# A split-precision transformer kernel on one core: weights in equal 1 MB chunks, with deeper slots and earlier splits

## The chip, the core and the metric

The kernel runs on one core of a Trainium2 chip. The metric is the device time of one execution in microseconds. A core has TensorE (PE in the profile), VectorE (DVE), ScalarE (ACT), GpSimd (POOL) and SyncE (SP), each with its own program; they meet at semaphores.

## What is computed

Two blocks on x of 256 tokens by 1024. The first has four layers (differential attention, stick-breaking attention, sliding-window attention, differential attention again), each followed by an output projection and a gated feed-forward network with a causal convolution; then a norm. The second has one layer with a pooling mixer beside attention, and at its end a gated embedding.

```python
for layer in range(DEPTH):                      # 4
    h = rmsnorm(x, attn_norm[layer])
    m = diff_attention | stick_breaking_attention | sliding_window_attention (h)
    x = x + m @ w_o[layer]
    h = rmsnorm(x, ffn_norm[layer])
    x = x + conv_gated_ffn(h, ffn_w_up[layer], ..., ffn_w_down[layer])
x = rmsnorm(x, final_norm)
# second block
proj = rms_norm(x, g_mix_pre) @ w_in
y = concat(pool_mixer(u), moba_attention(q, k, v)) @ w_out
x = x + rms_norm(y, g_mix_post)
x = x + rms_norm(conv_ffn(rms_norm(x, g_ffn_pre), w_up, conv_w, conv_b, w_down), g_ffn_post)
x = x + (p @ w_ple) * sigmoid(x @ w_ple_gate)
```

## The kernel before

All products are in fp32 made of two parts: every operand is rounded to a high half (type fp32r) and its remainder, the low half, and a product is three matmuls of 128x128 by 256 columns (`product`, L1568 to L1570) or, in the down stages of layers 0 to 3, one of 256 (L1578) and one of 512 columns (L1579, `wide_product`). The weights pass once through the core: SyncE loads a chunk from HBM into `w_raw`, ScalarE casts it into `w_hi` (L351), VectorE subtracts into `w_lo` (L863), TensorE multiplies. All three are rings of RING = 3 slots of 2816 columns. A chunk of an attention, wo or up stage is 2048 columns (1 MB), one of a down stage 2816 (one output tile, 22 units of 128 rows), one of the gate stage 2560.

The stages follow each other in the list `STAGES`: attention, wo, up, down for each of five layers, then gate. Every engine's program walks through it, and between its other work `next_split(c0, k)` casts or subtracts chunk c0+k+3, once TensorE has done with chunk c0+k (semaphore `used`, waited for by ScalarE). VectorE's program waits for `hi_ready`, SyncE's and TensorE's for `lo_ready`. TensorE begins a chunk with `chunk_ready` (L1583). A split is thus at a fixed place in each engine's program; where it stands, the engine's later work waits for it.

In a down stage VectorE adds each tile to x (L1369, L1372) as soon as TensorE is done with it, ScalarE squares the tile (L383, in down3 also L382), VectorE sums the squares into `acc` (L902, then L904) and subtracts the next chunk. TensorE does most of the first two tiles, then their rest once the last activations are there, and then one tile after the other. The split of the last tile is postponed until after the next normalisation.

A norm's statistic is a matmul of `acc` with ones (L1696) and of the last squares (L1700, `statistic`); TensorE has begun the next stage's first outputs by then, on x that is scaled but not normalised yet (h from `raw_high`, ACT L419, and `raw_low`, DVE L925). ScalarE makes rstd (L396), VectorE normalises (L916, low halves L912), for the chunks behind. In a wo stage the fourth chunk is split in halves (ACT L359, DVE L872), `added_to_x` adds the tiles (L1265), and the second and third splits stand among the squares. In layer 4 the result of wo is normed itself and then added (L1005, L1014), in a stage that the names call res_a.

In the attention groups of two heads (`group`), ScalarE makes exponentials (`exps`, L435), copies transposed probabilities (`copy_probT`, L443), and TensorE's `heads` (L1732) multiply these with the values. In the gate stage two `embedding` products stand ahead of the gate's first outputs. The repeating parts of the stages are hardware loops (`Fori`) on all engines.

## Time and profile before

| | |
|---|---|
| time of three runs | 1567.25, 1567.72, 1568.3 us (median 1567.72) |
| time of the profiled execution | 1566.53 us |
| its span in the profile | 1564.9 us |
| TensorE's matmuls (PE) | busy 1515.5 us, 11578 instructions |
| VectorE (DVE) | busy 1052.2 us |
| ScalarE (ACT) | busy 867.5 us |
| GpSimd (POOL) | busy 324.0 us |
| read from HBM | 262.50 MB |
| mean granted TensorE clock | 0.991 |

Times are microseconds from the start of the span. An engine is busy while it executes an instruction. A bracket at the end of a row of a timeline says how long the engine sat idle before and what released it. The difference between the execution's time and its span is 1.6 us.

### The profile page before, as it was taken

To read this page: it belongs to the slowest core of one execution; us is meant where nothing else is said; L and a number is where in the kernel's file an instruction comes from. 1 tells how busy PE (TensorE), PEld (TensorE's weight loads), DVE (VectorE), ACT (ScalarE), POOL (GpSimd) and SP (SyncE) were. 2 spreads that over 40 slices of the span, in tenths; PEclk is the share of its full clock that TensorE was granted. 3 is DMA by queue.
4 is the path that set the end of the run, shared out by engine and by line. 5 is a ranking of instruction groups with operands and counts; after the bars stand their busy time and mean duration, and the time that the engine had idled before them with its cause. 6 is when DMAs were issued, how large, how long until landed. Compare 5 with 4: busy or idle time off the path is not lost.

```text
span 1564.9 us, 31081 instructions
## 1 busy us (share of the span) xinstructions
PE 1515.5 (97%) x11578; PEld 1436.4 (92%) x11578; DVE 1052.2 (67%) x1677; ACT 867.5 (55%) x1365; POOL 324.0 (21%) x482
## 2 busy tenths in 40 slices
PE   8999999999999999989999999999999998899998
PEld 7989999899999998978999889889998887899998
DVE  6668877563378775666877576678785765866545
ACT  6766555465566554555656446666564555544533
POOL 2003212212222222212211221022112361211100
PEclk9999999999999999999999999999999998899999
DMA  7543656353336564442556545435564553455550
GB/s 263 185 149 115 209 187 240 139 186 116 126 108 215 183 223 158 161 163 81 195 182 222 180 165 172 150 127 201 182 233 148 170 173 108 143 182 196 192 208 28
DMA packets 37242, 264.65 MB, mean 169 GB/s; under 512 B 4959, under 2 KB 5274, under 8 KB 8496
## 3 DMA queue, kind: packets, MB, share of 16 engines
q1 hardware_dynamic: 33984, 255.54, 46.8%
q0 software_dynamic: 3040, 8.05, 2.0%
q8 instruction: 49, 0.80, 0.2%
q14 instruction: 25, 0.20, 0.0%
q10 hardware_dynamic: 144, 0.05, 0.0%
HBM read 262.50 MB, written 1.12 MB: 168 GB/s over the span
## 4 chain that ended last, share of the span: by engine, by line
PE 77%; DVE 13%; ACT 6%; issue 3%; DMA 1%; SPq 0%; ACTq 0%; POOL 0%; DVEq 0%
PE bank L1568 19%; PE bank L1569 19%; PE bank L1570 19%; PE bank L1579 9%; PE bank L1578 4%; DVE w_lo L863 4%; DVE tmp L916 2%; ACT w_hi L351 2%; ACT tmp L435 1%; PE bank L1617 1%; PE bank L1732 1%; DVE acc L904 1%; DVE tmp L948 1%; DVE h_lo L912 1%; DVE w_lo L872 1%
## 5 line engine op out<-in xcount | busy, mean ns | idle before, releaser
L863 DVE TENSOR_TENSOR w_lo<-w_raw,w_hi 128x2048 fp32r<-128x2048 f32 (+2 forms) x219 | 542.0, 2477 | 211.2 <-ACT w_hi L351 211.0
L1568 PE MATMUL bank<-h_hi,w_hi 128*128 128x256 f32 x2016 | 574.5, 285 | 2.2 <-DVE w_lo L863 2.2
L1569 PE MATMUL bank<-h_lo,w_hi 128*128 128x256 f32 x2016 | 570.4, 283 | 0.0
L1570 PE MATMUL bank<-h_hi,w_lo 128*128 128x256 f32 x2016 | 570.3, 283 | 0.0
L351 ACT CAST w_hi<-w_raw 128x2048 fp32r<-128x2048 f32 (+2 forms) x219 | 443.4, 2025 | 2.8 <-DVE proj L932 2.8
L1568 PEld LDWEIGHTS bank<-h_hi,w_hi 128*128 128x128 f32 x2016 | 386.5, 192 | 7.4 <-issue 3.5
L1569 PEld LDWEIGHTS bank<-h_lo,w_hi 128*128 128x128 f32 x2016 | 386.7, 192 | 0.1
L1570 PEld LDWEIGHTS bank<-h_hi,w_lo 128*128 128x128 f32 x2016 | 386.6, 192 | 0.0
L1579 PE MATMUL bank<-act_both,w_hi 128*128 128x512 f32 x704 | 248.9, 399 | 0.0
L800 ACT ACTIVATE tmp<-bank,par 128x256 f32<-128x256 f32 x181 | 93.4, 561 | 227.6 <-PE bank L1570 227.3
L1332 DVE SCALAR_TENSOR_TENSOR tmp<-bank,par,tmp 128x255 f32<-128x255 f32 (+1 forms) x362 | 155.4, 477 | 85.0 <-ACT tmp L800 82.3
L1578 PE MATMUL bank<-act_both,w_lo 128*128 128x256 f32 x704 | 197.7, 281 | 0.0
L1579 PEld LDWEIGHTS bank<-act_both,w_hi 128*128 128x128 f32 x704 | 132.3, 188 | 32.7
L1568 PE MATMUL bank<-act_both,w_hi 128*128 128x256 f32 x516 | 150.6, 292 | 6.7 <-DVE act_both L1020 5.1
L1569 PE MATMUL bank<-act_both,w_hi 128*128 128x256 f32 x516 | 146.6, 284 | 0.0
L1570 PE MATMUL bank<-act_both,w_lo 128*128 128x256 f32 x516 | 146.5, 284 | 0.0
L1539 POOL CAST act_both<-tmp 128x256 f32 x110 | 43.6, 397 | 481.0 <-DVE tmp L1349 371.1
L1578 PEld LDWEIGHTS bank<-act_both,w_lo 128*128 128x128 f32 x704 | 133.0, 189 | 0.0
L1568 PEld LDWEIGHTS bank<-act_both,w_hi 128*128 128x128 f32 x516 | 99.3, 192 | 13.2 <-DVE act_both L1020 7.0
L1617 PE MATMUL bank<-h_hi,w_hi 128*128 128x256 f32 x336 | 94.4, 301 | 5.9 <-ACT h_hi L419 2.9
L1569 PEld LDWEIGHTS bank<-act_both,w_hi 128*128 128x128 f32 x516 | 99.5, 193 | 0.1
L1570 PEld LDWEIGHTS bank<-act_both,w_lo 128*128 128x128 f32 x516 | 99.5, 193 | 0.0
(185 smaller groups left out, 2037.6 us busy)
## 6 DMA issues: line engine op xcount, KB each, us to landing
w_raw<-w_std SPq DMA_DIRECT2D x180, 1024.0 KB, 4.9
w_raw<-w_down SPq DMA_DIRECT2D x40, 1408.0 KB, 6.1
act_both<-vec_dram POOLq DMA_DIRECT2D x56, 128.0 KB, 3.6
w_raw<-w_gate SPq DMA_DIRECT2D x4, 1280.0 KB, 5.4
x<-xT SPq DMA_DIRECT2D x2, 512.0 KB, 6.0
out<-x SPq DMA_DIRECT2D x3, 256.0 KB, 2.3
w_raw<-w_std SPq DMA_DIRECT2D x2, 256.0 KB, 5.4
w_raw<-w_std SPq DMA_DIRECT2D x1, 512.0 KB, 8.0
```

What stands on the lines that cost most here:

```text
L351: act.copy(w_hi[:, slot, 0:width], w_raw[:, slot, 0:width]).then_inc(hi_ready, 1)
L800: act.activation(to[:, slot, :], source, ACT.Identity, bias=col(3), scale=col(2)).then_inc(conv_init, 1)
L863: dve.tensor_tensor(w_lo[:, slot, 0:width], w_raw[:, slot, 0:width], w_hi[:, slot, 0:width].bitcast(F32), ALU.subtract).then_inc(lo_ready, 1)
L916: dve.scalar_tensor_tensor(hf[:, k, :], x[:, k, :], gain_of(app, k), rstd[:, :], ALU.mult, ALU.mult).then_inc(hf_done, 1)
L1332: return dve.scalar_tensor_tensor(to[:, slot, lag:S], source(v)[:, 0:S - lag], par[:, bass.ds(at + (4 * v + 2 - lag), 1)], to[:, slot, lag:S],
L1539: pool.tensor_copy(act_hi[:, bass.ds(j, 1), :].squeeze(1) if not isinstance(j, int) else act_hi[rows, j, :], cval[rows, slot, :]).then_inc ...
L1568: pe.matmul(dst, wh, xh, start=first, stop=False, skip_group_check=shared)
L1569: pe.matmul(dst, wh, xl, start=False, stop=False, skip_group_check=shared)
L1570: done = pe.matmul(dst, wl, xh, start=False, stop=last, skip_group_check=shared)
L1578: pe.matmul(bank[:, 0:S], wl, xh, start=start and k == 0, stop=False, skip_group_check=True)
L1579: done = pe.matmul(bank[:, :], wh, pair, start=False, stop=stop and k == len(weights) - 1, skip_group_check=True)
L1617: pe.matmul(dst, a, b, start=k == 0 and w is wh and (n == 0 or not shared), stop=False, skip_group_check=shared)
```

## The change

All weights come in chunks of 1 MB: a down stage has 11 of them instead of 8 (a tile of 22 units crosses chunk borders), the gate's weights four and the embedding's one of its own. `w_raw` has three slots, `w_hi` and `w_lo` have SLOTS = 5. Splits are counted in chunks of weights: `split_to(c)` makes all that are missing up to c, and `ahead(c, lead)` those up to lead beyond the stage's chunk c. ScalarE's lead is mostly one more than VectorE's (`HIGH`, `high_up`, `low_up`); in down both are at 5. ScalarE waits for `used` of the chunk that had the slot. In the last group of an attention stage both engines make extra splits; a wo stage has one split, behind the first addition to x, and one after the normalisation; nothing is split in halves and nothing postponed. In `group`, `copy_probT(s, 0)` stands ahead of the next exponentials. In the gate stage all four embeddings stand first. All hardware loops are written out. New lines: splits ACT L363 and DVE L841, additions in down DVE L1326 and L1329, sums of squares DVE L870 and L872, in wo L1232, `product` PE L1522 to L1524, `wide_product` PE L1532 and L1533.

```diff
@@ -58,17 +56,33 @@
 
 
 STAGES = []
-SIZES = []
-for _kind, _count, _width in (
-        ("da", 12, STD), ("wo", 4, STD), ("up", FT, STD), ("down", DT, DOWN),
-        ("sb", 12, STD), ("wo", 4, STD), ("up", FT, STD), ("down", DT, DOWN),
-        ("sw", 6, STD), ("wo", 4, STD), ("up", FT, STD), ("down", DT, DOWN),
-        ("da", 12, STD), ("wo", 4, STD), ("up", FT, STD), ("down", DT, DOWN),
-        ("mix", 9, STD), ("wo", 4, STD), ("up", FT, STD), ("down", DT, DOWN),
-        ("gate", 4, GATE)):
-    STAGES.append((_kind, len(SIZES), _count))
-    SIZES += [_width] * _count
-CHUNKS = len(SIZES)
+_at = 0
+for _kind, _count in (
+        ("da", 12), ("wo", 4), ("up", FT), ("down", DT),
+        ("sb", 12), ("wo", 4), ("up", FT), ("down", DT),
+        ("sw", 6), ("wo", 4), ("up", FT), ("down", DT),
+        ("da", 12), ("wo", 4), ("up", FT), ("down", DT),
+        ("mix", 9), ("wo", 4), ("up", FT), ("down", DT),
+        ("gate", 4)):
+    STAGES.append((_kind, _at, _count))
+    _at += _count
+SLOTS = 5
+AHEAD = 5
+HIGH = 4
+RAW = 3
+UNITS = STD // P
+DOWN = FT * DT // UNITS
+
+
+WEIGHTS = []
+FIRST_WEIGHTS = {}
+for _kind, _first, _count in STAGES:
+    FIRST_WEIGHTS[_first] = len(WEIGHTS)
+    if _kind == "down":
+        WEIGHTS += [_first + (UNITS * _j + UNITS - 1) // FT for _j in range(DOWN)]
+    else:
+        WEIGHTS += ([_first] if _kind == "gate" else []) + [_first + _j for _j in range(_count)]
+CHUNKS = len(WEIGHTS)
 EXP_AND_LN = 6
 WINDOWS = (2, 4, 8, 16)
...
 
+        def weights_of(layer, c):
+
+            return c + (DOWN - DT) * layer + (layer == 5)
+
+        def weight_slot(layer, c):
+            return weights_of(layer, c) % SLOTS
+
+        def high_up(j):
+
+            return min(AHEAD, RING + (j + 1) // 2)
+
+        def low_up(j):
+
+            return min(AHEAD - 1, RING + j // 4)
+
+        def down_weights(c0, k):
+
...
+            split = [1]
+
+            def split_to(c):
+
+                for n in range(split[0], min(c + 1, CHUNKS)):
+                    if n >= SLOTS:
+                        act.wait_ge(used, WEIGHTS[n - SLOTS] + 1)
+                    act.wait_ge(arrived[n % RAW], n // RAW * 16 + 16)
+                    act.copy(w_hi[:, n % SLOTS, :], w_raw[:, n % RAW, :]).then_inc(hi_ready, 1)
+                    split[0] = n + 1
+
+            def ahead(c, lead=RING):
+
+                split_to(weights_of(layer, c) + lead)
 
...
@@ -560,13 +550,13 @@
 
                             q, s, d, t = (i * 2 + half, i * 2 + s_half, i * 2 + d_half, i * 2 + first_tile)
                             at = i * RING + (g0 + RING)
-                            reg = i if not isinstance(i, int) else None
-                            off = g0 + RING + (i * RING if isinstance(i, int) else 0)
+                            copy_probT(s, 0, maps)
                             exps(s + 1, 1, 0)
                             if more:
                                 evac_qk(at, slot_of(g0, 0), 0)
-                            copy_probT(s, 0, maps)
                             head_squares(q, d, 0) if da else mix_high(q, t)
+                            if not more and da:
+                                ahead(c0 + n, HIGH)
                             if not more and not da:
                                 act.wait_ge(used, at + 1)
                                 for g in range(4):
@@ -574,20 +564,20 @@
...
@@ -736,19 +727,13 @@
                             for k in tiles:
                                 raw_high(app, k)
 
-                    split_hi_halves(c0)
-                    if layer < 4:
-                        next_split(c0, 1)
+                    ahead(c0, AHEAD)
                     squared(0)
                     raw(0, 1)
                     squared(1)
-                    if layer == 4:
-                        next_split(c0, 1)
...
-                n = c0 + k + RING
-                if i is None and n >= CHUNKS:
-                    return
-                split_lo(n if i is None else i * RING + n, n % RING, SIZES[n])
+            split = [1]
+
+            def split_to(c):
+
+                for n in range(split[0], min(c + 1, CHUNKS)):
+                    dve.wait_ge(hi_ready, n + 1)
+                    dve.tensor_tensor(w_lo[:, n % SLOTS, :], w_raw[:, n % RAW, :],
+                                      w_hi[:, n % SLOTS, :].bitcast(F32), ALU.subtract).then_inc(lo_ready, 1)
+                    split[0] = n + 1
+
...
@@ -1266,10 +1233,9 @@
                            .then_inc(x_part if k == 3 else bank_free, 1)
 
                     added_to_x(0)
-                    split_lo_halves(c0, layer)
+                    ahead(c0, AHEAD)
                     added_to_x(1)
                     added_to_x(2)
-                    next_split(c0, 1)
                     for j in range(3):
                         add_squares(name, j)
                         if layer < 4:
@@ -1279,19 +1245,16 @@
                     if layer < 4:
                         raw_low(app, 6)
                         raw_low(app, 7)
-                        next_split(c0, 2)
                         normalise(app, SUMS[name][2])
-                        next_split(c0, 3)
...
@@ -1302,7 +1265,7 @@
                         dve.wait_ge(conv_part, (j + ffn * FT) * 3 + 3)
                         dve.scalar_tensor_tensor(cgate[:, slot, 2:S], pj[slot][:, 0:S - 2], par[:, at:at + 1],
                                                  cgate[:, slot, 2:S], ALU.mult, ALU.add).then_inc(bank_free, 1)
-                        next_split(c, 0)
+                        split_to(weights_of(layer, c) + low_up(j))
                         dve.wait_ge(gated, j + ffn * FT + 1)
                         dve.tensor_tensor(cval[0:HALF, slot, :], cgate[0:HALF, slot, :], cval[0:HALF, slot, :],
...
@@ -1376,7 +1333,7 @@
                         if layer < 4 and raw_engine(app, k):
                             raw_low(app, k)
                         if k < DT - 1:
-                            next_split(c0, k)
+                            split_to(down_weights(c0, k) + AHEAD)
                     if layer == 4:
                         dve.wait_ge(p_hi, 1)
...
-                    def down(c, slot, a=0, b=FT):
-
+                    first = FIRST_WEIGHTS[c0]
+
+                    def down_tile(f, k):
+
+                        n, at = divmod(f * FT + k, UNITS)
+                        return w_tile((first + n) % SLOTS, at, P, 0)
+
+                    def down(f, a=0, b=FT):
+
+                        pe.wait_ge(lo_ready, first + (f * FT + b - 1) // UNITS + 1)
                         if a == 0:
-                            chunk_ready(c)
-                        weights = [w_tile(slot, k, P, 0) for k in range(a, b)]
+                            pe.wait_ge(bank_free, c0 + f + 1)
+                        bank = pj[slot_of(c0, f)]
+                        weights = [down_tile(f, k) for k in range(a, b)]
                         if layer < 4:
...
@@ -2062,32 +2017,33 @@
                     layer += 1
                 else:
                     def embedding(k):
-                        slot = slot_of(c0, k)
+
+                        for t in range(2):
+                            done = product(embedded[k][:, t * S:t * S + S],
+                                           [w_tile(ple % SLOTS, 2 * k + f, 2 * P, t * P) for f in range(2)],
+                                           [(act_hi[:, f, :], act_lo[:, f, :]) for f in range(2)])
+                        return done
+
+                    ple = FIRST_WEIGHTS[c0]
+                    pe.wait_ge(lo_ready, ple + 1)
+                    pe.wait_ge(p_lo, 1)
+                    for k in range(4):
+                        embedding(k)
+                    for k in range(n):
+                        slot, weights = slot_of(c0, k), weight_slot(layer, c0 + k)
                         chunk_ready(c0 + k)
-                        for t in range(2):
-                            product(val_bank[k % 3][:, t * S:t * S + S],
-                                    [w_tile(slot, DT + f, 2 * P, t * P) for f in range(2)],
-                                    [(act_hi[:, f, :], act_lo[:, f, :]) for f in range(2)])
-
-                    pe.wait_ge(p_lo, 1)
```

VectorE, wo stage of layer 0, from the first addition to x to the first of the normalisation (L1265/L1232 adds to x, L904/L872 sum squares, L925/L893 low halves of h). Before:

```order
L872 TENSOR_TENSOR w_lo<-w_raw,w_hi 128x1024 [waits half_hi]
L872 TENSOR_TENSOR w_lo<-w_raw,w_hi 128x1024 [waits hi_ready]
L1265 TENSOR_TENSOR x<-bank,x 128x512 [waits used] x2
L863 TENSOR_TENSOR w_lo<-w_raw,w_hi 128x2048 [waits hi_ready]
L904 TENSOR_TENSOR acc<-sq 128x256 [waits acc_done,sq_ready]
L925 SCALAR_TENSOR_TENSOR h_lo<-x,par,h_hi 128x256 [waits raw_hi]
L904 TENSOR_TENSOR acc<-acc,sq 128x256 [waits acc_done,sq_ready]
```

```order
L1265 TENSOR_TENSOR x<-bank,x 128x256 [waits tile6_done]
L1265 TENSOR_TENSOR x<-bank,x 128x256 [waits used]
L925 SCALAR_TENSOR_TENSOR h_lo<-x,par,h_hi 128x256 [waits raw_hi] x2
L863 TENSOR_TENSOR w_lo<-w_raw,w_hi 128x2048 [waits hi_ready]
L916 SCALAR_TENSOR_TENSOR tmp<-x,par,rstd 128x256 [waits rstd_done]
```

And now:

```order
L1232 TENSOR_TENSOR x<-bank,x 128x512 [waits used]
L841 TENSOR_TENSOR w_lo<-w_raw,w_hi 128x2048 [waits hi_ready]
L1232 TENSOR_TENSOR x<-bank,x 128x512 [waits used] x2
L872 TENSOR_TENSOR acc<-sq 128x256 [waits acc_done,sq_ready]
L893 SCALAR_TENSOR_TENSOR h_lo<-x,par,h_hi 128x256 [waits raw_hi]
L872 TENSOR_TENSOR acc<-acc,sq 128x256 [waits acc_done,sq_ready]
```

```order
L893 SCALAR_TENSOR_TENSOR h_lo<-x,par,h_hi 128x256 [waits raw_hi]
L1232 TENSOR_TENSOR x<-bank,x 128x256 [waits tile6_done]
L1232 TENSOR_TENSOR x<-bank,x 128x256 [waits used]
L893 SCALAR_TENSOR_TENSOR h_lo<-x,par,h_hi 128x256 [waits raw_hi] x2
L884 SCALAR_TENSOR_TENSOR tmp<-x,par,rstd 128x256 [waits rstd_done]
```

Of four splits between the first addition and the normalisation (two halves, two whole) one whole is left, in the halves' place.

VectorE, the start of the down stage of layer 0, behind the last row of up. Before:

```order
L1307 TENSOR_TENSOR tmp<-tmp 64x256 [waits gated]
L1369 TENSOR_TENSOR x<-bank,x 128x256 [waits used]
L1372 TENSOR_TENSOR x<-bank,x 128x256 [waits x_main]
L902 COPY acc<-sq 128x256 [waits acc_done,sq_ready]
L863 TENSOR_TENSOR w_lo<-w_raw,w_hi 128x2816 [waits hi_ready]
L1369 TENSOR_TENSOR x<-bank,x 128x256 [waits used]
L1372 TENSOR_TENSOR x<-bank,x 128x256 [waits x_main]
```

And now:

```order
L1270 TENSOR_TENSOR tmp<-tmp 64x256 [waits gated]
L1326 TENSOR_TENSOR x<-bank,x 128x256 [waits used]
L1329 TENSOR_TENSOR x<-bank,x 128x256 [waits x_main]
L870 COPY acc<-sq 128x256 [waits acc_done,sq_ready]
L841 TENSOR_TENSOR w_lo<-w_raw,w_hi 128x2048 [waits hi_ready] x2
L1326 TENSOR_TENSOR x<-bank,x 128x256 [waits used]
L1329 TENSOR_TENSOR x<-bank,x 128x256 [waits x_main]
```

The third tile's weights were a chunk split in up; now they end in the stage's fifth chunk, the first of the two L841 behind the COPY. TensorE, end of the second tile and start of the third (its first row waits for `bank_free` and `lo_ready`), now:

```order
L1533 MATMUL bank<-act_both,w_hi 128x512
L1532 MATMUL bank<-act_both,w_lo 128x256
L1533 MATMUL bank<-act_both,w_hi 128x512
L1532 MATMUL bank<-act_both,w_lo 128x256 [waits bank_free,lo_ready]
L1533 MATMUL bank<-act_both,w_hi 128x512
```

ScalarE, last group of the mix layer (L435/L433 exponentials, L443/L441 the copy, L449/L447 heads' results, L574/L564 the pooled). Before:

```order
L483 COPY vtok<-bank 128x512 [waits pv_done,used]
L351 CAST w_hi<-w_raw 128x2048 [waits arrived2,used]
L435 ACTIVATE tmp,small<-tmp,small 128x128 [waits nmax_ready]
L435 ACTIVATE tmp,small<-tmp,small 128x256
L435 ACTIVATE tmp,small<-tmp,small 128x128
L435 ACTIVATE tmp,small<-tmp,small 128x256
L443 COPY tmp<-bank 128x384 [waits trans_done]
L443 COPY tmp<-bank 128x384
L449 CAST act_both<-bank 128x256 [waits pv_done]
L574 ACTIVATE act_both<-bank,par 128x256 [waits used]
```

And now:

```order
L481 COPY vtok<-bank 128x512 [waits pv_done,used]
L363 CAST w_hi<-w_raw 128x2048 [waits arrived0,used]
L441 COPY tmp<-bank 128x384 [waits trans_done]
L441 COPY tmp<-bank 128x384
L433 ACTIVATE tmp,small<-tmp,small 128x128 [waits nmax_ready]
L433 ACTIVATE tmp,small<-tmp,small 128x256
L433 ACTIVATE tmp,small<-tmp,small 128x128
L433 ACTIVATE tmp,small<-tmp,small 128x256
L447 CAST act_both<-bank 128x256 [waits pv_done]
L564 ACTIVATE act_both<-bank,par 128x256 [waits used]
```

The copy for the first head moved ahead of the four exponentials of the second, and stands right behind the cast.

## Rows read from the trace of the kernel before

**Rows 1.** The page: part 1 (busy time), part 4 (chain), shares by engine.

```profile
PE 1515.5 (97%) x11578; PEld 1436.4 (92%) x11578; DVE 1052.2 (67%) x1677; ACT 867.5 (55%) x1365; POOL 324.0 (21%) x482
...
PE 77%; DVE 13%; ACT 6%; issue 3%; DMA 1%; SPq 0%; ACTq 0%; POOL 0%; DVEq 0%
```

**Rows 2.** Timeline of PE, gate stage; start us, us, engine line op, [idle before <-releaser].

```profile
1533.52 0.28 PE L1617 MATMUL bank<-h_hi,w_hi 128*128 128x256 f32 x1
1533.64 0.28 PE L1617 MATMUL bank<-h_hi,w_lo 128*128 128x256 f32 x1
```

**Rows 3.** Timeline of PE, first down stage: the third tile's first matmuls.

```profile
276.39 0.28 PE L1578 MATMUL bank<-act_both,w_lo 128*128 128x256 f32 x1
...
276.75 0.28 PE L1578 MATMUL bank<-act_both,w_lo 128*128 128x256 f32 x1
```

**Rows 4.** PE's waits, whole span; us in total, times, longest us.

```profile
PE bank L1732 <- ACT tmp L443: 6.5, 6, 1.6
PE bank L1696 <- DVE acc L904: 5.7, 5, 2.0
...
PE bank L1700 <- ACT sq L383: 5.0, 5, 2.2
PE bank L1568 <- DVE w_lo L863: 4.2, 9, 0.6
...
PE bank L1626 <- DVE h_lo L912: 1.6, 6, 0.4
...
PE bank L1568 <- DVE w_lo L872: 0.2, 1, 0.2
```

**Rows 5.** Timeline of PE, layer 0's attention, first and last group.

```profile
46.17 0.45 PE L1732 MATMUL bank<-tmp,vtok 128*128 128x256 f32 x1 [0.80 <-ACT tmp L443]
...
111.76 0.45 PE L1732 MATMUL bank<-tmp,vtok 128*128 128x256 f32 x1 [1.25 <-ACT tmp L443]
```

**Rows 6.** Timelines of ACT and PE, last group of the mix layer.

```profile
1290.88 0.46 ACT L443 COPY tmp<-bank 128x384 f32<-128x384 f32 x1
...
1291.81 0.70 PE L1732 MATMUL bank<-tmp,vtok 128*64 128x256 f32 x2 [2.42 <-issue]
```

**Rows 7.** Timeline of DVE, wo of layer 0.

```profile
128.11 2.28 DVE L863 TENSOR_TENSOR w_lo<-w_raw,w_hi 128x2048 fp32r<-128x2048 f32 x1
```

**Rows 8.** Groups of DVE by form: busy us, mean ns, idle before.

```profile
L863 DVE TENSOR_TENSOR w_lo<-w_raw,w_hi 128x2048 fp32r<-128x2048 f32 x175 | 405.0, 2317 | 134.7 <-ACT w_hi L351 134.4
L863 DVE TENSOR_TENSOR w_lo<-w_raw,w_hi 128x2816 fp32r<-128x2816 f32 x40 | 125.8, 3144 | 68.9 <-ACT w_hi L351 68.9
```

**Rows 9.** Timeline of DVE, wo of layer 4.

```profile
1329.02 2.29 DVE L863 TENSOR_TENSOR w_lo<-w_raw,w_hi 128x2048 fp32r<-128x2048 f32 x1 [0.75 <-ACT w_hi L351]
```

**Rows 10.** Timeline of PE, gate stage: the last of the first 48 matmuls.

```profile
1540.71 0.40 PE L1626 MATMUL bank<-h_lo,w_hi 128*128 128x256 f32 x2
```

**Rows 11.** Windows; busy us of PE, PEld, DVE, ACT, POOL, then PEclk, DMA share, GB/s.

```profile
448.10:451.80 3.70, 2.11 (x10) 1.08 (x8) 2.89 (x7) 2.30 (x5) 2.58 (x4) 1.00 0.40 168
451.90:455.20 3.30, 3.30 (x16) 3.21 (x16) 3.30 (x5) 2.89 (x4) 0.00 (x0) 0.50 0.00 0
1291.80:1294.90 3.10, 3.09 (x15) 2.46 (x16) 1.02 (x4) 1.50 (x5) 0.00 (x0) 0.50 0.76 254
1229.00:1231.80 2.80, 0.73 (x2) 0.00 (x0) 2.02 (x3) 0.71 (x2) 0.93 (x2) 1.00 1.01 198
152.00:266.00 114.00, 114.00 (x939) 113.35 (x938) 90.72 (x125) 68.15 (x84) 23.32 (x42) 1.00 0.59 201
```

**Rows 12.** Timeline of DVE: first tile's squares in down, layers 0 and 4.

```profile
276.90 0.29 DVE L902 COPY acc<-sq 128x256 f32<-128x256 f32 x1 [0.48 <-ACT sq L383]
...
1480.44 0.29 DVE L902 COPY acc<-sq 128x256 f32<-128x256 f32 x1 [8.71 <-ACT sq L383]
```

**Rows 13.** Timeline of PE, down of layer 4: the third tile's start.

```profile
1481.02 0.28 PE L1569 MATMUL bank<-act_both,w_hi 128*128 128x256 f32 x1
```

**Rows 14.** Timeline of ACT, first group of layer 1's attention.

```profile
342.60 1.91 ACT L351 CAST w_hi<-w_raw 128x2048 fp32r<-128x2048 f32 x1
```

404 lines of the change are left out of this document (154 added, 250 removed).

## The prediction

> **What bounds the kernel now.** I began with the busy shares and the chain of waits [rows 1]. TensorE is busy for 1515.5 of 1564.9 us, and 77% of the chain is TensorE's own work, 19% is VectorE's and ScalarE's. The matmuls are the same before and after, so only the time that TensorE does not spend at full rate can change. Beside each other, 256-column matmuls start every 0.12 us [rows 2]. In the down stages of the first four layers, a pair (256 and 512 columns) takes 0.36 us [rows 3]. Then the list of TensorE's waits [rows 4] says what it waited for: attention copies, the statistic of a norm, low halves of weights. I take each of them in turn. The profiled execution took 1566.53 us, 1.2 below the median of 1567.72; the sum goes by it, and 1.2 is added at the end. About 0.2% (3.1 us) is what a measurement can tell from no change.
>
> **What should be gained.**
> 1. Attention groups. In the differential layers ScalarE now copies the first transposed probabilities ahead of the next exponentials. The three waits of TensorE for that copy [rows 4, 5] are 0.80 in the first group of layer 0, 1.25 in its last and 1.6 in layer 3; I keep 0.3 for what is next in line and take 3.4. In the last group of the mix layer the copy stands behind four exponentials: it starts at 1290.88, TensorE's heads at 1291.81 after a wait of 2.42 [rows 6]. The copy needs only the transposes, which had ended at 1288.4. I take 2.4, and 0.8 (half) of what the slow clock behind this wait costs (below): 3.2.
> 2. The wo stages of layers 0 to 3. VectorE has a split of 2.28 at 128.11 ahead of the statistic's sums [rows 7] and another just ahead of the normalisation (order of VectorE ahead, first place); neither is there any more. TensorE waited for the sums 0.9 in each of the four layers (5.7 in five waits less the 2.0 of wo4) and for the last squares 0.7 each (5.0 less the 2.2 of down3) [rows 4], 6.5 in all. Next in line is the addition of the last tile to x and its square, which stay; I leave 0.3 per layer to them and take 5.2. Of the 1.6 for low halves of h (L912) I take 1.1.
> 3. Weights that come late. Nine waits for w_lo of L863 and one of L872 make 4.4 [rows 4]: the third chunk after a down stage, whose split was postponed, and the third chunk of up, whose split follows the normalisation. With five slots both are split well ahead: 4.4.
> 4. At the end of down3 a 2816-column subtraction (3.14) [rows 8] stands in each tile's round, and the last squares come 2.2 late [rows 4]. The pieces are now 2048 wide (2.32), and the last round has one or none of them: 2.6, with the idle piece behind it.
> 5. wo4: a cast and then a subtraction (2.29 after 0.75 idle) [rows 9] stand in VectorE's chain of x, sums and h; they are gone, and the chain is what all waits there hang on: 3.0.
> 6. The end: the gate's first 48 matmuls run from 1533.52 [rows 2] to 1540.95, two starts after the last row's [rows 10], where 48 x 0.12 is 5.8: they wait for h. Two more embeddings (24 matmuls, 2.9) now stand ahead and fill these 1.7.
> 7. Clock: 451.90 to 455.20 ran at a granted clock of 0.50 [rows 11], the 1.2 GHz level, after TensorE had been busy 2.11 of the 3.70 us before. At half clock matmuls start every 0.213 us, so 3.3 us do the work of 1.8: 1.5 lost, and gained once the two waits before it are.
>
> Sum: 3.4 + 3.2 + 5.2 + 1.1 + 4.4 + 2.6 + 3.0 + 1.7 + 1.5 = 26.1.
>
> **What should be lost.**
> 1. **A new wait at the third tile of every down stage.** Tile 2 needs units 44 to 65, that is chunks 2 to 4 of the stage. Up leaves four of them subtracted; the fifth follows on VectorE only behind the first tile's two additions and the COPY of its squares (order of VectorE ahead, second place). In the trace of before these end at 276.90 + 0.29 = 277.2 [rows 12], for they wait for the first tile's matmuls. Then comes a subtraction of 2.3 (the 2048-wide mean is 2.32): 279.5. TensorE begins tile 2 at 276.39 [rows 3] (44 pairs after the stage's first). So 3.1 us in each of layers 0 to 2; in layer 3 the squares are two ACTIVATEs, 0.6 more, 3.7; in layer 4 the COPY ends at 1480.73 [rows 12], the subtraction at 1483.0, and TensorE gets there at 1481.0 [rows 13]: 2.0. In all 3 x 3.1 + 3.7 + 2.0 = 15.0. Before, tile 2 had a chunk of its own that was ready, so no wait. ScalarE's cast is no help: it is done in up already. The next tile is safe: its chunk is the second subtraction, ready 2.3 later, while tile 2 takes 22 x 0.36 = 7.9.
> 2. The slow clock behind these waits. No row shows a wait of 3.1 after a long dense stretch. The nearest: after the 2.42 before 1291.8 the clock was 0.50 for 3.1 us, after 2.8 us with 0.73 busy (1229.0 to 1231.8) it stayed 1.00 [rows 11]. Bounds 0 and 5 x 1.5 = 7.5; I take three of five, 4.5. The Trainium skill (TensorE: Matmul & The Clock Gate, "The HAM clock gate") says that an idle TensorE falls to 1.2 GHz and must be kept fed; by it alone all five would fall and the loss would be 7.5, and the rows so far show it after some gaps and not after others.
> 3. Stick-breaking's first group: its cast of 1.9 right ahead of the logarithms [rows 14] is two casts now. TensorE has the first chunks of group 1 to do meanwhile, so of 1.9 some 1.1 should show (0 to 1.9).
>
> Sum: 15.0 + 4.5 + 1.1 = 20.6.
>
> **What costs nothing.** Loads: some 240 loads of 1 MB instead of 225 of 1 to 1.4 MB; each waits for a slot far ahead of need, and TensorE's list has no wait for weights from memory. The splits that move into the last heads lie where VectorE waits for the last squares and heads (it idles for a third of the span); if that cover were gone, each would cost up to 2.3 before wo, 11.5 at most over five stages. The five w_hi and w_lo slots: without price. Unrolling: in the up stage of layer 0, with its loop turns, 939 recorded matmuls take 114.0 us [rows 11], and 939 x 0.12 is 112.7, so at most 1.3 us are there to gain. I take 0.
>
> Net 26.1 - 20.6 = 5.5 less: 1561.0 on the profiled execution, **1562.2** on the median.
>
> **Rivals.**
> - *The down wait shows nothing* (the fifth chunk is ready by another way than I read, or TensorE is late there for another reason): 1562.2 - 15.0 - 4.5 = 1542.7. Against it: the wait on lo_ready stands in the program and VectorE's order is fixed. Chance 0.09.
> - *Slower: the gains at the statistics fall to the next in line.* In wo0 to wo3 and at down3 and wo4 the last addition to x, its square and the copy to acc follow each other across VectorE and ScalarE, and cutting 2.3 us of split ahead of them gains only if they start earlier. If the last matmuls set their start, gain terms 2 (5.2 + 1.1), 4 and half of 5 fall away, 10.4, and with all five clocks down 3.0 more is lost: 1562.2 + 13.4 = 1575.6. It decides slower once 8.7 (1570.9 - 1562.2) of the gains are missing. For it: L1265 adds the last two tiles behind TensorE's own last matmuls of wo. Against: the wait for the sums (0.9) came before. Chance 0.13.
> - *Unrolling pays.* If each of the five up stages had 1.3 to give, it would be 1562.2 - 6.5 = 1555.7. The Trainium skill (Runtime: NRT & Kernel Launch, "Instruction fetch mechanics") says that a taken branch outside the two pages held breaks the sequential prefetch and that unrolling avoids it; no gap stands at a loop's turn here. Chance 0.08.
> - *The clock alone is misjudged*: none or all of the five: 1557.7 or 1565.2. Chance 0.20, in both cases with my mechanism.
> - The forecast as it stands: 0.50.
>
> **How the numbers follow.** The forecast's own bounds: 0 to 1.9 for the logarithms, 0 to 7.5 for the clock, and the gains to within a fifth (5) give 1553 to 1571. The slower rival with half its price ends at 1569; a quarter of the cases beyond either end is left out, so 1550 to 1572. Faster (below 1564.6): the first rival, the third, half of the clock's and 0.35 of the forecast's 0.50, 0.62. Slower (above 1570.9): 0.13. The same: 0.25.
>
> **What would show it.** In the profile after: a wait of the 256-column matmul for w_lo at the third tile of each down stage, about 3.1 four times and 2.0 in layer 4, and PEclk 0.5 behind some of them. The waits for acc and for w_lo at the third chunks are gone, the wait of the heads for the copy of the probabilities too. VectorE's split stands at 2.32 mean with no 3.14. I would be wrong if the down stages had no wait, or if TensorE still waited for sums in wo.

## The result, and the profile after

The changed kernel takes 1571.19 us (median of 19 runs, 1566.15 to 1572.51), the kernel before 1568.3 us beside it (19 runs, 1566.78 to 1570.06). The ratio is 1.0015, with an interval from 1.0009 to 1.0021: slower by some 2.4 us. That is little, but it lies clear of 1 on the side that I had not forecast: I had forecast 1562.2, or 5.5 less. The profiled execution took 1569.87 us with a span of 1568.2.

The page after, its span, busy times and chain:

```profile
span 1568.2 us, 28431 instructions
...
PE 1515.6 (97%) x11578; PEld 1440.5 (92%) x11578; DVE 1053.3 (67%) x1688; ACT 868.8 (55%) x1376; POOL 337.0 (21%) x482
...
PE 82%; DVE 8%; ACT 6%; issue 2%; POOL 1%; DMA 1%; SPq 0%; ACTq 0%
```

TensorE's work is as before [rows 1]: 1515.6 us of 11578 matmuls. GpSimd's 324.0 has become 337.0, though it does the same 482 instructions: its masks in the stick-breaking layer took 17.9 us and take 22.2, and its scalings of x (L1441 before, L1395 now), for which no wait of TensorE is listed, took 47.7 and take 60.0. TensorE's waits after (line, what it waited for; us in total, times, longest):

```profile
PE bank L1532 <- DVE w_lo L841: 12.1, 4, 3.4
PE bank L1834 <- POOL tmp L1467: 8.0, 6, 2.4
PE bank L1522 <- DVE act_both L988: 5.0, 3, 2.2
...
PE bank L1522 <- DVE w_lo L841: 4.1, 7, 1.9
PE bank L1689 <- ACT tmp L441: 3.1, 5, 1.1
...
PE bank L1657 <- ACT sq L381: 1.9, 4, 0.5
PE bank L1653 <- DVE acc L872: 1.9, 2, 1.2
```

Against [rows 4]: the copy of the probabilities (L443, 6.5 us) is at 3.1, the sums (L904, 5.7) at 1.9, the last squares (L383, 5.0) at 1.9, and the wait of 2.42 in the mix layer [rows 6] is gone (0.3 of issue is left of it). Two waits are new: 12.1 us for the low halves of weights at the third tile of four down stages (L1532; layer 4's own, 1.9, is in the L1522 row of 4.1), and 8.0 us for GpSimd's masks in the stick-breaking layer (L1834). The first I had forecast. The second I had not: in the kernel before it is 0.7 us.

The forecast wait, in the down stage of layer 0 (VectorE's COPY and its two subtractions, then TensorE's third tile):

```profile
272.01 0.29 DVE L870 COPY acc<-sq 128x256 f32<-128x256 f32 x1 [0.48 <-ACT sq L381]
272.22 4.49 DVE L841 TENSOR_TENSOR w_lo<-w_raw,w_hi 128x2048 fp32r<-128x2048 f32 x2
...
274.56 0.38 PE L1532 MATMUL bank<-act_both,w_lo 128*128 128x256 f32 x1 [2.90 <-DVE w_lo L841]
```

The COPY ends at 272.30, the first subtraction at 274.50, and TensorE starts at 274.56 after 2.90 idle. The five waits are 2.90 in layers 0 to 2, 3.43 in layer 3 and 1.93 in layer 4. Behind four of them TensorE's clock is halved. Windows of the trace after, columns as in [rows 11]:

```profile
600.60:604.00 3.40, 3.40 (x12) 2.91 (x11) 1.93 (x4) 1.94 (x3) 3.02 (x4) 0.50 0.93 371
883.90:887.30 3.40, 3.40 (x12) 2.88 (x11) 2.88 (x4) 0.75 (x3) 3.27 (x2) 0.50 0.84 279
1191.10:1194.50 3.40, 3.40 (x12) 2.92 (x11) 2.48 (x4) 1.44 (x4) 2.71 (x3) 0.50 0.87 330
1484.60:1488.00 3.40, 3.40 (x18) 3.40 (x17) 3.40 (x3) 1.39 (x1) 0.00 (x0) 0.50 0.86 287
274.40:277.80 3.40, 3.24 (x19) 2.87 (x20) 3.06 (x4) 0.27 (x1) 3.32 (x2) 1.00 0.70 212
```

The four windows at 0.50 are at 1.2 GHz, the last of them behind the wait of only 1.93; the one behind the first wait is not, although that wait is 2.90. In the whole trace 10 stretches add up to 41.3 us at half clock; before they were 7 with 29.7.

The other new wait, second group of the stick-breaking layer. VectorE's softplus (L1169) and subtraction (L841), GpSimd's masks (L1467), TensorE:

```profile
375.04 1.02 DVE L1169 SCALAR_TENSOR_TENSOR tmp<-bank,tmp 128x384 f32<-128x384 f32 x2 [1.39 <-ACT tmp L625]
375.98 2.28 DVE L841 TENSOR_TENSOR w_lo<-w_raw,w_hi 128x2048 fp32r<-128x2048 f32 x1
...
375.67 3.58 POOL L1467 TENSOR_SCALAR_AFFINE_SELECT tmp<-tmp 128x256 f32<-128x256 f32 x4 [1.54 <-DVE tmp L1169]
...
378.58 0.48 PE L1834 MATMUL bank<-tmp,cst 128*128 128x256 f32 x1 [1.41 <-POOL tmp L1467]
```

The same place before (L1206 is the softplus, L1513 the masks, then ScalarE's cast):

```profile
373.70 1.02 DVE L1206 SCALAR_TENSOR_TENSOR tmp<-bank,tmp 128x384 f32<-128x384 f32 x2 [1.19 <-ACT tmp L636]
...
374.33 0.87 POOL L1513 TENSOR_SCALAR_AFFINE_SELECT tmp<-tmp 128x256 f32<-128x256 f32 x2 [1.34 <-DVE tmp L1206]
376.35 0.79 POOL L1513 TENSOR_SCALAR_AFFINE_SELECT tmp<-tmp 128x256 f32<-128x256 f32 x2 [1.14 <-ACT tmp L643]
...
376.54 1.90 ACT L351 CAST w_hi<-w_raw 128x2048 fp32r<-128x2048 f32 x1
```

Before, the two masks behind the softplus take 0.87 us, and the next two at 376.35 take 0.79. After, VectorE starts the subtraction at 375.98, in the middle of the masks, and the row of masks from 375.67 is 3.58 long. The instruction alone, over all groups (ns min/median/max), after:

```profile
L1467 POOL TENSOR_SCALAR_AFFINE_SELECT tmp<-tmp x32: 402/407/2397, 345.6 to 433.6; 128x256 f32<-128x256 f32 x32
```

The median is 0.407 us, the longest 2.397. In each of the four groups one mask begins 0.15 us after a subtraction of 2.28 or 2.29 has begun, takes 2.39 to 2.40 and ends 0.26 after it; two more begin 1.30 after one and take 1.25, again to 0.26 after its end. So a mask that begins while a subtraction runs stands still until the subtraction is over. A mask that was already running when one began (348.02, the subtraction at 348.33) took its 0.41.

### The profile page after: what moved, and what is told of

The parts are those of the page before. It is cut to its first block, busy times and chain, and to the rows that moved or that the text cites. A ratio compares the mean times of both kernels' runs of the same rounds, so it can differ in the third digit from the quotient of the medians.

```text
span 1568.2 us, 28431 instructions
## 1 busy us (share of the span) xinstructions
PE 1515.6 (97%) x11578; PEld 1440.5 (92%) x11578; DVE 1053.3 (67%) x1688; ACT 868.8 (55%) x1376; POOL 337.0 (21%) x482
## 4 chain that ended last, share of the span: by engine, by line
PE 82%; DVE 8%; ACT 6%; issue 2%; POOL 1%; DMA 1%; SPq 0%; ACTq 0%
PE bank L1522 20%; PE bank L1524 19%; PE bank L1523 19%; PE bank L1533 10%; PE bank L1532 5%; ACT w_hi L363 2%; DVE w_lo L841 2%; PE bank L1571 2%; DVE tmp L884 2%; PE bank L1580 1%; PE bank L1689 1%; DVE acc L872 1%; POOL tmp L1467 1%; ACT tmp L433 1%; PE bank L1657 1%
## 5 line engine op out<-in xcount | busy, mean ns | idle before, releaser
L841 DVE TENSOR_TENSOR w_lo<-w_raw,w_hi 128x2048 fp32r<-128x2048 f32 x240 | 556.5, 2326 | 91.8 <-ACT w_hi L363 91.6
L1522 PE MATMUL bank<-h_hi,w_hi 128*128 128x256 f32 x2016 | 574.8, 285 | 1.9 <-DVE w_lo L841 1.9
L1524 PE MATMUL bank<-h_hi,w_lo 128*128 128x256 f32 x2016 | 570.5, 283 | 0.0
L363 ACT CAST w_hi<-w_raw 128x2048 fp32r<-128x2048 f32 x240 | 454.5, 1903 | 73.1 <-DMA w_raw<-w_std 59.6
L1522 PEld LDWEIGHTS bank<-h_hi,w_hi 128*128 128x128 f32 x2016 | 386.8, 192 | 7.1 <-issue 3.5
L1524 PEld LDWEIGHTS bank<-h_hi,w_lo 128*128 128x128 f32 x2016 | 386.7, 192 | 0.0
L1533 PE MATMUL bank<-act_both,w_hi 128*128 128x512 f32 x704 | 251.8, 401 | 0.0
L1532 PE MATMUL bank<-act_both,w_lo 128*128 128x256 f32 x704 | 200.0, 284 | 12.1 <-DVE w_lo L841 12.1
L1533 PEld LDWEIGHTS bank<-act_both,w_hi 128*128 128x128 f32 x704 | 134.3, 191 | 31.9
L1522 PE MATMUL bank<-act_both,w_hi 128*128 128x256 f32 x516 | 150.8, 292 | 7.8 <-DVE act_both L988 5.0
L1532 PEld LDWEIGHTS bank<-act_both,w_lo 128*128 128x128 f32 x704 | 135.3, 192 | 13.4 <-DVE w_lo L841 13.4
L1524 PE MATMUL bank<-act_both,w_lo 128*128 128x256 f32 x516 | 146.9, 285 | 0.0
L1522 PEld LDWEIGHTS bank<-act_both,w_hi 128*128 128x128 f32 x516 | 99.8, 193 | 13.4 <-DVE act_both L988 6.3
L381 ACT ACTIVATE sq<-x 128x256 f32<-128x256 f32 (+1 forms) x62 | 29.3, 474 | 139.9 <-DVE x L1329 119.2
L1395 POOL TENSOR_SCALAR proj<-x,par 128x256 f32<-128x256 f32 x33 | 49.8, 1509 | 255.3 <-ACT h_hi L417 254.8
```

The lines of the kernel that those rows point to most:

```text
L363: act.copy(w_hi[:, n % SLOTS, :], w_raw[:, n % RAW, :]).then_inc(hi_ready, 1)
L841: dve.tensor_tensor(w_lo[:, n % SLOTS, :], w_raw[:, n % RAW, :], w_hi[:, n % SLOTS, :].bitcast(F32), ALU.subtract).then_inc(lo_ready, 1)
L1395: pool.tensor_scalar(proj[:, k % 4, :], x[:, k, :], gain_of(app, k), None, ALU.mult)\
L1522: pe.matmul(dst, wh, xh, start=first, stop=False, skip_group_check=shared)
L1524: done = pe.matmul(dst, wl, xh, start=False, stop=last, skip_group_check=shared)
L1532: pe.matmul(bank[:, 0:S], wl, xh, start=start and k == 0, stop=False, skip_group_check=True)
```

## The experiments

Each one was timed beside the kernel before; ratios are to that kernel, differences are of medians, "against the changed kernel" means against its 1571.19.

### The fifth subtraction of down ahead of the additions

```diff
                 elif kind == "down":
                     name = f"down{layer}"
+                    split_to(FIRST_WEIGHTS[c0] + AHEAD - 1)
                     for k in range(DT):
```

> The changed kernel, with VectorE's fifth subtraction of each down stage moved ahead of the stage's first addition (it stood behind the first tile's additions and the COPY of its squares). My theory: the wait of TensorE at the third tile (12.1 us in four waits and 2.1 in layer 4) goes entirely and with it four stretches of half clock (4 x 1.5 us): 14.9 + 6 = some 19 to 21 us less than the changed kernel, ratio to the kernel before about 0.989. Rival A, that ScalarE's casts or the loads set that chunk: the wait stays at 2 us or more per stage and the time moves by less than 5. Rival B, that the half clock comes anyway: 15 less, and the stretches near 600, 884, 1191 and 1485 stay.

Measured: 1549.64 us, ratio 0.9871 (0.9856 to 0.9886), 21.5 less than the changed kernel. VectorE at the start of down now:

```profile
270.59 0.42 DVE L1327 TENSOR_TENSOR x<-bank,x 128x256 f32<-128x256 f32 x1 [6.34 <-PE bank L1534]
271.05 0.42 DVE L1330 TENSOR_TENSOR x<-bank,x 128x256 f32<-128x256 f32 x1
271.95 0.29 DVE L870 COPY acc<-sq 128x256 f32<-128x256 f32 x1 [0.48 <-ACT sq L381]
274.16 2.29 DVE L841 TENSOR_TENSOR w_lo<-w_raw,w_hi 128x2048 fp32r<-128x2048 f32 x1 [1.91 <-ACT w_hi L363]
```

No subtraction that the third tile needs stands behind the COPY any more; what comes at 274.16 is the sixth chunk. Of TensorE's waits none for w_lo is left at the wide products; those for the masks are as they were, and the other ones for w_lo are without layer 4's:

```profile
PE bank L1835 <- POOL tmp L1468: 8.1, 6, 2.4
...
PE bank L1523 <- DVE w_lo L841: 1.9, 5, 0.4
```

The four stretches of half clock are gone with the waits (the trace has 6 left, 24.2 us). My theory holds, rivals A and B fall. The gaps at the third tiles, beyond the usual spacing of matmuls, were 3.06 three times, 3.59 and 2.09, or 14.9; with four stretches of 3.4 us at half speed (an estimate of 1.5 each, 6.0) that is 20.9 of the 21.5. The spans of the two profiled executions differ by 20.2.

### VectorE's subtractions behind the masks

```diff
                             softplus(b, 0)
                             softplus(b, 1)
+                            mix_low(q, i * 2)
                             if more:
                                 ahead(at)
                                 ahead(at + 1)
                             else:
                                 ahead(c0 + n)
                                 ahead(c0 + n, HIGH)
-                            mix_low(q, i * 2)
                             mix_low(q + 1, i * 2 + 1)
```

> The changed kernel, with VectorE's two subtractions in each stick-breaking group moved from ahead of the first low half of the heads' results to behind it; ScalarE's order is untouched. Theory: GpSimd's masks (0.41 us alone, up to 2.40 in the changed kernel) stand still while VectorE subtracts 2048 columns beside them; with the subtraction behind, masks take 0.41 again and TensorE's 8.0 us of waits for them go, with one half-clock stretch (1.5): 8 to 9.5 less than the changed kernel, ratio to before about 0.996. Rival, that ScalarE's extra cast ahead of the logarithms delays the masks: the waits of about 1.6 to 2.5 per group stay, time the same within 2 us.

`mix_low` makes the low half of a head's result; its first call now stands between the softplus and the subtractions.

Measured: 1560.29 us, ratio 0.9948 (0.9934 to 0.9961), 10.9 less. The masks in this kernel:

```profile
L1467 POOL TENSOR_SCALAR_AFFINE_SELECT tmp<-tmp x32: 406/406/410, 348.0 to 427.8; 128x256 f32<-128x256 f32 x32
```

Every one takes 0.41. TensorE's waits for them fell from 8.0 to 1.7 us. ScalarE's order is that of the changed kernel, casts ahead of the logarithms included, so the rival falls as the main cause.

### ScalarE's lead back to three in the stick-breaking groups

```diff
                             if more:
-                                ahead(at, HIGH)
+                                ahead(at)
...
                             if more:
-                                ahead(at + 1, HIGH)
+                                ahead(at + 1)
...
-                                ahead(at + 2, HIGH)
+                                ahead(at + 2)
...
-                        ahead(g0 + 2, HIGH)
+                        ahead(g0 + 2)
```

> The changed kernel, with ScalarE's lead in the stick-breaking groups back from four chunks to three; VectorE's order is untouched, and its subtraction waits for the cast as before. Theory of the masks: the subtraction can't start before the masks are done, so the masks are short and TensorE's 8.0 us of waits go: 8 to 9.5 less, ratio about 0.996. If only one of this run and of the one with VectorE's subtractions moved brings it, the order of ScalarE (this one) or the overlap (the other) is the cause; if both do, it is the overlap.

Measured: 1559.61 us, ratio 0.994 (0.9927 to 0.9954), 11.6 less. TensorE's wait for masks is 0.6 us. Here VectorE's order is untouched. Both moves bring it, and what they share is that the subtraction no longer meets the masks that TensorE waits for. From the first to the last matmul that waited for masks in the changed kernel (346.53 to 430.65, 84.1 us) the same matmuls now take 74.4, 9.7 less: 7.2 of waits, the stretch of half clock at 351.4 (an estimate of 1.5), and the rest not told apart. The other 1.9 of the 11.6 fell elsewhere.

This also says where the overlap came from. In the kernel before VectorE's subtraction stood at the same place in its program, but it waited for a cast that ScalarE began at 376.54 (above) and ended at 378.45; the two masks from 376.35 were done by 377.14. The subtraction then ran from 378.48 and stalled the next mask, for which TensorE did not wait. The lead of four had the cast done early, the wait on `hi_ready` was over before it began, and the subtraction ran at once, into the masks that TensorE waits for.

### The loops of the kernel before written out

```diff
-                            with act.Fori(0, groups - 1) as i:
+                            for i in range(0, groups - 1):
```

and so at all loops of TensorE, ScalarE and VectorE.

> The kernel before with the hardware loops of TensorE, ScalarE and VectorE written out, as in the change, and nothing else. My forecast: no difference, 0 within 2 us (ratio 0.999 to 1.001), since no gap stood at a loop's turn. Rival, that turns cost: 4 to 8 us less. Rival, that the longer program costs (twice the instruction fetches): 2 to 5 more.

Measured: 1567.77 us, ratio 0.9991 (0.9982 to 1.0), 0.9 less. At most a small gain; the rival of 4 to 8 falls, and so does a cost of 2 to 5. The two profiled executions differ by more than that inside: TensorE's waits add up to 41.1 us against 45.2 before, and its half clock to 40.8 us against 29.7. So the 0.9 is what is left of both; the price of the loops without the clock was not measured.

### The copy of the probabilities first, in the kernel before

```diff
+                            copy_probT(s, 0, maps)
                             exps(s + 1, 1, 0)
                             if more:
                                 evac_qk(at, slot_of(g0, 0), 0)
-                            copy_probT(s, 0, maps)
```

> The kernel before with only the copy of the first head's transposed probabilities put ahead of the next exponentials. My terms for this part: 3.4 in the differential layers and 3.2 in the mix layer, 6.6 less, ratio 0.996, with the wait of 2.42 at 1291.8 and its half clock gone. Rival: the exponentials behind the copy are late in turn and TensorE waits for the divided probabilities instead: within 2 us of before.

Measured: 1562.03 us, ratio 0.9963 (0.995 to 0.9977), 6.2 less. TensorE's waits for the copy, 6.5 before:

```profile
PE bank L1732 <- ACT tmp L443: 2.8, 3, 1.1
```

The wait of 2.42 in the mix layer is gone and no stretch of half clock stands behind it. A wait of 1.2 for divided probabilities (L987) is new, the rival in small.

### Both repairs together

> The changed kernel with both repairs: the fifth subtraction of a down stage ahead of its additions, and ScalarE's lead of three in the stick-breaking groups. If the two losses are independent, their measured savings add up (21.5 and 11.6 by the medians of their own runs against the changed kernel's 1571.2): 1538, ratio to before 0.981. If each saving held part of the other's clock stretches, 1541 to 1543.

Its edits are those of the first and the third experiment. Measured: 1539.59 us, ratio 0.9819 (0.9805 to 0.9832). The two savings alone add up to 33.1; together they are 31.6. So they are nearly independent. The profiled execution took 1541.18. TensorE's longest waits in this kernel:

```profile
PE bank L1572 <- ACT h_hi L413: 3.9, 2, 2.1
PE bank L1523 <- DVE act_both L988: 3.4, 2, 2.2
PE bank L1690 <- ACT tmp L441: 3.1, 5, 1.1
...
PE bank L1523 <- DVE w_lo L841: 2.4, 6, 0.4
...
PE bank L1835 <- POOL tmp L1468: 0.6, 2, 0.4
```

### One cast less ahead of the first norm

```diff
-            split_to(2)
+            split_to(1)
...
                     if c0 == 0:
+                        split_to(2)
                         act.wait_ge(lam_dots, 4)
```

> The kernel with both repairs, and ScalarE's cast of the third chunk of the whole program moved from ahead of the first norm's rstd to behind the first high halves. TensorE waits 2.4 us for those high halves at 20.3 in the changed kernel. Theory: that wait ends about 1.9 (one cast) sooner, 1.5 to 2 us less than with both repairs. Rival: the third chunk itself becomes late (its low half is needed at about 32), nothing gained or 1 us lost.

Measured: 1540.48 us, ratio 0.9822 (0.9809 to 0.9836), 0.9 more than with both repairs alone and within their intervals. The wait for h did not get shorter (3.8 in two waits, against 3.9), and those for low halves of weights grew from 2.4 to 3.3. At TensorE's first wait for weights, at 28 us, it is 0.9 behind. Nothing gained, the rival's result.

### One split back among the squares of wo

```diff
                     squared(1)
+                    if layer < 4:
+                        ahead(c0 + 1, AHEAD)
                     raw(2, 3)
...
                     added_to_x(2)
+                    if layer < 4:
+                        ahead(c0 + 1, AHEAD)
                     for j in range(3):
```

> The kernel with both repairs, and in the wo stages of layers 0 to 3 one more cast and one more subtraction put back ahead of the sums of squares (before: two; the change left one). Theory: the waits of TensorE for the sums (about 1.0 each, gone in three of four layers of the changed kernel) come back, and those for the low half of the third chunk of up (0.5 each) go: 4 x (1.2 - 0.55), 2 to 4 us more. Rival, that the sums were set by TensorE's own last matmuls all along: 2 us less, by the 0.5 each.

Measured: 1558.18 us, ratio 0.9931 (0.9917 to 0.9944), 18.6 more than with both repairs, where I had expected 2 to 4. The waits for sums and for the low halves of h that come before them:

```profile
PE bank L1658 <- DVE acc L874: 12.9, 5, 2.6
...
PE bank L1585 <- DVE h_lo L895: 3.7, 4, 1.5
```

Four of the five waits for sums are of some 2.6, where the kernel before had 0.9; and in each of the four stages the clock is halved for 6.8 us, where in the kernel before it was once, for 3.4 (at 451.9). The window at the first:

```profile
132.40:139.20 6.80, 5.18 (x16) 4.09 (x17) 4.50 (x11) 2.82 (x8) 1.20 (x2) 0.50 0.25 101
```

Per stage the waits for sums (2.6) and for low halves of h (0.7, in layer 2 1.5) are new in place of those for the last squares (0.5), the third chunk (0.4) and, in layer 2, the sums (0.65): 2.5 more. The other 2.1 of the 4.65 measured (18.6 / 4) go with the clock: in the four windows of 6.8 us TensorE is busy for 5.3 on average, and at 1.5 lost in 3.4 busy ones that would be 2.3, an estimate. The trace shows where my size went wrong. ScalarE's cast stands here between the second squares and the third (125.74 to 127.63), VectorE's subtraction waits for it (127.66 to 129.95), and the first sum starts at 129.87 where it started at 125.81 with both repairs: cast and subtraction both lie in the chain. In the kernel before the casts stood ahead of the first squares. The direction, that a split ahead of the sums costs time, is shown; that the order of the kernel before costs less was not run by itself.

### ScalarE's lead back to three in the other groups

The same edit as in the stick-breaking groups, in those of the differential and mix layers.

> The kernel with both repairs, and ScalarE's lead in the groups of the differential and mix layers back to three chunks as well. If a lead of four by itself buys something there (low halves that no longer wait for a cast), this is 1 to 3 us slower than with both repairs; if it is only neutral there and harmful where GpSimd's masks stand beside it, the same within 1 us.

Measured: 1546.41 us, ratio 0.9853 (0.9838 to 0.9868), 6.8 more than with both repairs. TensorE's waits for the copy went from 3.1 to

```profile
PE bank L1690 <- ACT tmp L441: 6.3, 5, 1.8
```

with two of 1.8 in the last groups of the differential layers, where two casts stand in front of the copy, not one. The spans of the profiled executions differ by 5.5. The waits of the mix layer are unchanged. So a lead of four is worth its place in the differential layers, more than I had expected, and harmful in the stick-breaking layer alone.

### Two embeddings back behind the gate's first outputs

```diff
-                    for k in range(4):
+                    for k in range(2):
                         embedding(k)
                     for k in range(n):
                         slot, weights = slot_of(c0, k), weight_slot(layer, c0 + k)
+                        if k > 1:
+                            embedding(k)
```

> The kernel with both repairs, and the third and fourth embedding products put back behind the gate's first outputs, as before the change. My term for moving them was 1.7: so 1.7 slower than with both repairs (1 to 2). Rival, that the end is set by the casts and loads of the gate's chunks: no difference.

Measured: 1543.09 us, ratio 0.9835 (0.9821 to 0.9848), 3.5 more by the medians. The two profiled executions differ by 1.9 in their spans (1541.5 and 1539.5), all of it behind the last norm's statistic. The term of 1.7 holds by the span. The other 1.6 of the medians is the distance of the profiled execution with both repairs (1541.18) from its own median (1539.59); here all executions lie between 1542.83 and 1543.23.

### Rounding ahead of the exponentials in the sliding-window layer

```diff
+                            mix_high(q, j)
                             if j < 6:
                                 exps(s + 2, j % 2, j + 3)
-                            mix_high(q, j)
```

> The kernel with both repairs, and in the sliding-window layer ScalarE rounds a head pair's result (the high half that wo multiplies) ahead of the next exponentials, the same kind of move as the copy of the probabilities. TensorE waits there 3.4 us in two waits for the low halves that follow it, and 6.8 us run at half clock beside it. Theory: 1.5 to 2 of the first wait of 2.46 and perhaps one clock stretch (1.5) go, 2 to 3 less than with both repairs. Rival: the exponentials come late in turn, and the waits for the divided probabilities grow by as much: the same.

On top of both repairs. Measured: 1538.12 us, ratio 0.9804 (0.9791 to 0.9817), 1.5 less than with both repairs, at the edge of what the runs tell apart. The wait of 2.2 (683.29 with both repairs) is gone and so are the 6.8 us of half clock there, but 2 us later TensorE waits 2.8 for the copy of the probabilities instead of 0.8, and its waits for the copy grew from 3.1 to 5.5 in sum: theory and rival both in part. It is the fastest kernel of this study, 31 us below the one before.

## Why the prediction was wrong

The end of my sum was a difference of two large numbers, 26.1 gained and 20.6 lost. The experiments give both: with the two losses repaired the kernel is 28.6 below before (1568.18 to 1539.59), and the losses together are 31.6. The difference is 3.0 on the slow side, as measured (2.4 by the ratio). The gains were right in sum (28.6 against 26.1), partly because misses of single terms cancel (below); the losses were 31.6 against 20.6.

**The step that failed** is loss 3, "of 1.9 some 1.1 should show (0 to 1.9)". It took in only the second cast ahead of the first group's logarithms [rows 14]. The part cost 11.6 us, ten times as much (9.7 of it inside the layer's groups), and by another mechanism: what VectorE did while GpSimd masked. The casts themselves may have cost what I gave them: with only VectorE's order changed, TensorE waits 1.7 for masks, with ScalarE's lead back at three 0.6. I had looked for what the earlier casts would delay on ScalarE's own queue, and not for what they would release: VectorE's subtraction, four times, each time next to GpSimd's masks. The trace of before held the warning: GpSimd's mask has a maximum of 2129 ns there over a median of 407, in the three that met a subtraction where nobody waited:

```profile
L1513 POOL TENSOR_SCALAR_AFFINE_SELECT tmp<-tmp x32: 402/407/2129, 347.4 to 427.0; 128x256 f32<-128x256 f32 x32
```

and my bound of 1.9 excluded it without a reason. The Trainium skill (SBUF — State Buffer, "Who interferes with whom") says that a VectorE tensor-tensor operation with both inputs in SBUF contends with GpSimd's reads at ports that the two share, that whichever issues first holds them, and that the other is blocked fully. The masks of 2.40 us that began behind a subtraction agree with it, and so does a subtraction that began behind a mask (351.28, below).

**Loss 1, the third tile of down**: right in place, mechanism and size. Forecast 3.1, 3.1, 3.1, 3.7, 2.0, in sum 15.0; measured 3.06 three times, 3.59 and 2.09, in sum 14.9. Moving one subtraction made it go.

**Loss 2, the clock behind them**: forecast three of five, measured four (600.6, 883.9, 1191.1, 1484.6), so 6.0 against 4.5, by the same estimate of 1.5 each. Taken as halving the clock behind every wait, the rule in the prediction was one off. That I took three was a choice between bounds, so its nearness to four is luck. Removing the wait removed all four. In the kernels with the other repair alone it was three and four of five, at other stages.

**Gain 1, attention groups**: forecast 6.6, alone on the kernel before 6.2. In the changed kernel the three waits of the differential layers, 3.7 before, are two of 0.16; taking the lead of four away cost 6.8, a part that my terms didn't have. In the mix layer the 2.42 is 0.28, and a wait of 1.18 for divided probabilities has come behind it.

**Gain 2, wo**: forecast 5.2 and 1.1. The waits for sums and last squares in these four layers were 6.5 and are 2.6 (0.7 of sums, 1.9 of squares), so 3.9 (my term: 6.5 less 4 times 0.3 is 5.3, not 5.2). Of the 1.6 for low halves of h only 0.65 stood in these stages, the rest at the program's start (0.67) and behind down3 (0.32); so I could not have had 1.1 there. The sum of the two is 4.5 against 6.3. The rival that these gains fall to the next in line falls.

**Gain 3, weights that come late**: forecast 4.4, half wrong. The third chunk after a down stage no longer waits, but the third chunk of up still does: its subtraction stands behind the normalisation as before. Of the 4.1 us after, 1.9 is layer 4's third tile, 2.2 is left of 4.4, so 2.2 was gained.

**Gain 4, down3**: the 2.2 wait for the last squares isn't in the list after (its longest is 0.5). Forecast 2.6.

**Gain 5, wo4**: from one statistic to the next it took 17.9 us before (1319.88 to 1337.78) and 15.0 after (1324.01 to 1338.97), 2.9 less; forecast 3.0.

**Gain 6, the end**: from the last statistic to the end 36.5 before and 35.0 after, 1.5; and 1.9 by the experiment. Forecast 1.7.

**Gain 7, the clock of 451.9**: no stretch there after.

Only gains 1 and 6, and of gain 2 one split put back, had a run of their own; the others are differences between the two profiles.

**Costs of nothing**: the written-out loops, 0.9 us by the medians, with the interval of the ratio reaching 1. That loads and splits in the last heads cost nothing was right except in the stick-breaking layer's last group, where the two extra subtractions met the masks as well.

The forecast had slower at 0.13, for a rival that did not happen; that the measured time fell inside 1550 to 1572 is owed to the width of that range. Its low end was added wrongly: 1562.2 less 1.1, 4.5 and 5 is 1551.6, not 1553. Had the overlap been priced at one subtraction of 2.3 in each of the four groups, 9.2 instead of 1.1, the sum would have come out 2.6 slower, and the 9.2 is near the 9.7 measured inside the groups.

## What to carry to other kernels

When an engine is made to run ahead, ask what its semaphore had been holding back: an operation that waited for it now starts at once, beside other neighbours than before. Read the minimum, median and maximum of an instruction on GpSimd: a maximum several times the median says that it meets something, and in the next schedule somebody may be waiting for it. And where a forecast is a small difference of two large sums, the sign hangs on the smallest term that was not measured; bound such a term by what each engine beside it does.

## What the runs showed of the hardware

A mask of GpSimd (128x256, fp32) took 0.402 us alone and up to 2.397 when it began beside a running 128x2048 subtraction on VectorE, whose own time stayed at 2.28 to 2.29. It goes the other way too. Rows of the trace after: a subtraction that began 0.09 us behind the second mask of a pair took 2.46, and one that began 0.07 behind another operation of GpSimd with two inputs took 2.82, as did five more like it.

```profile
350.83 0.76 POOL L1467 TENSOR_SCALAR_AFFINE_SELECT tmp<-tmp 128x256 f32<-128x256 f32 x2
351.28 2.46 DVE L841 TENSOR_TENSOR w_lo<-w_raw,w_hi 128x2048 fp32r<-128x2048 f32 x1 [0.67 <-ACT w_hi L363]
25.14 0.75 POOL L1383 TENSOR_TENSOR h_lo<-tmp,h_hi 128x256 fp32r<-128x256 f32 x1 [0.80 <-ACT h_hi L413]
25.21 2.82 DVE L841 TENSOR_TENSOR w_lo<-w_raw,w_hi 128x2048 fp32r<-128x2048 f32 x1
```

In the kernel with the lead of three the maximum is 2129 ns again, and nobody waits for those masks:

```profile
L1467 POOL TENSOR_SCALAR_AFFINE_SELECT tmp<-tmp x32: 401/406/2129, 345.4 to 425.0; 128x256 f32<-128x256 f32 x32
```

Waits of TensorE of 1.9 to 3.4 us between dense stretches of down were followed by 3.4 us at half clock in four of five cases of the changed kernel, the shortest (1.93) among them and one of 2.90 (ending at 274.56) not. With the lead of three that same wait ended at 274.42 and was followed by half clock, and the one of the next layer was not. So the length of the wait alone does not decide it. In the kernel with a split among the squares, waits of 2.6 us came with 6.8 us at half clock in all four wo stages.
